# Gate and up projections of two feed-forwards by seven block products instead of eight

## The reference

```python
D_FF = ((8 * D_MODEL // 3 + 255) // 256) * 256        # 2816

def swiglu(x, w_gu, w_down):
    gu = x @ w_gu
    g, u = jnp.split(gu, 2, axis=-1)
    return (jax.nn.silu(g) * u) @ w_down

x = x + 0.5 * swiglu(rms_norm(x, g_ffn1[layer]), w_ffn1_gu[layer], w_ffn1_down[layer])
...
x = x + 0.5 * swiglu(rms_norm(x, g_ffn2[layer]), w_ffn2_gu[layer], w_ffn2_down[layer])
return rms_norm(x, g_final)
```

## Time and profile before

| | us |
|---|---|
| median of 3 runs | 1751.66 (1751.65 to 1751.79) |
| the profiled execution | 1754.53 |
| its span, first to last instruction | 1752.7 |
| PE busy in the span | 1742.0 (99%) |
| DVE / ACT / POOL busy | 1039.4 / 760.7 / 431.9 |

### The profile page before, as it was taken

One profiled execution on the slowest core, in us unless ns is written; L12 is line 12 of the kernel. 1 busy time (PEld: TensorE's weight loads), 2 busy tenths in 40 slices (PEclk: granted clock), 3 DMA queues, 4 the chain that ended last, 5 costly groups with the idle time before them and its releaser, 6 DMA issues.

```text
span 1752.7 us, 25465 instructions
## 1 busy us (share of the span) xinstructions
PE 1742.0 (99%) x9322; PEld 1437.8 (82%) x9322; DVE 1039.4 (59%) x2178; ACT 760.7 (43%) x1413; POOL 431.9 (25%) x336
## 2 busy tenths in 40 slices
PE   9999999999999999999999999999999999999998
PEld 7778878777888888888888888889888888888887
DVE  5888867688867665555433455446756655555332
ACT  6566645556654533333232454555444322333222
POOL 4566644465553500000000332320200200000000
PEclk9999999999999999999999999999999999999999
DMA  6422123332212433333333422223321333333332
GB/s 198 138 88 73 60 61 98 95 95 79 73 49 62 138 109 96 96 96 96 106 101 106 151 64 93 85 84 103 103 64 58 96 96 96 96 96 96 109 107 85
DMA packets 54998, 166.20 MB, mean 95 GB/s; under 512 B 10264, under 2 KB 10776, under 8 KB 54904
## 3 DMA queue, kind: packets, MB, share of 16 engines
q1 hardware_dynamic: 53896, 163.69, 30.8%
q10 hardware_dynamic: 1008, 1.28, 0.2%
HBM read 162.25 MB, written 2.17 MB: 94 GB/s over the span
## 4 chain that ended last, share of the span: by engine, by line
PE 99%; DMA 0%; DVE 0%; ACT 0%; POOL 0%; SPq 0%; issue 0%; POOLq 0%
PE proj L1182 80%; PE turned L1514 2%; PE o L1536 2%; PE proj L1678 1%; PE proj L1671 1%; PE o L1779 1%; PE o L1879 1%; PE turned L1148 1%; PE turned L1758 1%; PE score L1483 1%; PE score L1868 1%; PE turned L1741 1%; PE score L1472 1%; PE score L1348 0%; PE proj L1382 0%; PE score L1741 0%
## 5 line engine op out<-in xcount | busy, mean ns | idle before, releaser
L1182 PE MATMUL proj<-hhi,whi 128*128 128x512 f32 x1456 | 580.8, 399 | 0.0
L1182 PE MATMUL proj<-hhi,wlo 128*128 128x512 f32 x1456 | 568.4, 390 | 0.0
L1182 PE MATMUL proj<-hlo,whi 128*128 128x512 f32 x1456 | 567.4, 390 | 0.0
L1970 ACT ACTIVATE whi<-ring 128x1024 fp32r<-128x1024 f32 x278 | 294.2, 1058 | 613.6 <-PE proj L1182 593.8
L2495 DVE TENSOR_TENSOR wlo<-ring,whi 128x1024 fp32r<-128x1024 f32 x199 | 243.0, 1221 | 161.7 <-ACT whi L1970 161.2
L1182 PEld LDWEIGHTS proj<-hhi,whi 128*128 128x128 f32 x1456 | 274.0, 188 | 61.3 <-issue 7.3
L1182 PEld LDWEIGHTS proj<-hhi,wlo 128*128 128x128 f32 x1456 | 273.4, 188 | 58.8
L1182 PEld LDWEIGHTS proj<-hlo,whi 128*128 128x128 f32 x1456 | 274.1, 188 | 53.0
L884 POOL TENSOR_TENSOR wlo<-ring,whi 128x512 fp32r<-128x512 f32 x160 | 213.9, 1358 | 331.7 <-ACT whi L1970 331.4
L902 POOL TENSOR_TENSOR prob<-prob 128x512 f32<-128x512 f32 x36 | 56.8, 1579 | 871.2 <-ACT prob L1966 871.2
L1996 ACT ACTIVATE prob<-prob,negmax 128x128 f32<-128x128 f32 (+3 forms) x208 | 114.0, 550 | 80.5 <-DVE negmax L2568 80.1
(11 more groups left out here) (402 smaller groups left out, 2470.1 us busy)
## 6 DMA issues: line engine op xcount, KB each, us to landing
ring<-wstream SPq DMA_DIRECT2D x285, 512.0 KB, 3.6
arena<-lines SPq DMA_DIRECT2D x28, 256.0 KB, 5.4
out<-arena SPq DMA_DIRECT2D x8, 256.0 KB, 3.3
arena<-x ACTq DMA_DIRECT2D x4, 256.0 KB, 5.5
arena<-x SPq DMA_DIRECT2D x4, 256.0 KB, 6.2
arena<-mem SPq DMA_DIRECT2D x1, 1024.0 KB, 8.7
ring<-wstream SPq DMA_DIRECT2D x12, 64.0 KB, 2.3
ring<-wstream SPq DMA_DIRECT2D x2, 256.0 KB, 7.3
```

The costliest lines, as they stand in the source:

```text
L1182: mm = pe.matmul(b, rounded(w), rounded(rhs(v, k)), start=(first and n == 0 and p == 0), stop=(last and n == len(blocks) - 1 and p == 2))
L1970: act.activation(rounded(dst), src, ACT.Copy, scale=scale).then_inc(ready, 1)
```

## The change

Chunks 0 and 1 of each feed-forward stay as they are (PEEL = 2). For the other 20 (SEVEN), gate weights and up weights of a chunk are seen as one matrix of 2 x 2 blocks: gate and up by the first and second tile of each pair of input tiles. The normalised input, too, is 2 x 2 blocks: the two tiles of a pair by positions 0-255 and 256-511 (HALF_S). The product of these takes eight block products; the change uses the form with seven, in which some products are of sums of blocks:

- of weights: S1 (two up blocks), S2 (S1 and a gate block), S3 (gate and up), S4 (S2 and a gate block), made for every chunk by POOL in `seven_sums`; A11, A12 and A22 are used as they are,
- of inputs: T1 to T4 from `hx` (x times the gain, eight ACT copies in `scale_h`), made once per feed-forward by DVE (`combine_h`), rounded by ACT, low parts of T1 and T2 by POOL and of T3 and T4 by DVE.

Each of the seven products is 4 tile pairs x 3 parts = 12 matmuls of 128x256, in the order A11, S1, S2, A12, S3, S4, A22. Three banks hold the results: X (`proj`), Y (`score`), Z (`opsum`). X is continued by S2, S3 and A22, so ACT copies X after A11, S2 and S3 and Z after S1 (`q1c`, `v2c`, `v3c`, `q5c`), and DVE makes three adds. The high parts of the seven weight operands are made by ACT (`high_w`), the low parts of S2 and S3 by POOL, those of A11, S1, A12, A22 and S4 by DVE (`low_w`). The gating (`gated`) is done one chunk late. SP loads a chunk's two slots once DVE has made the low part of A22 of the chunk before last, not by jobs. `norm_first` goes behind the loop, and the loading of the first `bias2` rows (`load_bias2`) too.

```diff
+PEEL = 2
+SEVEN = FC - PEEL
+W_A11, W_S1, W_S2, W_A12, W_S3, W_S4, W_A22 = range(7)
+T_1, T_2, T_3, T_4 = range(4)
+HALF_S = S // 2
...
+        hx = over("hx", "arena", [P, KC, S], inner_at + 12 * S)
+        tsum, tlo = over("tsum", "yT", [P, 4, D]), over("tlo", "yT", [P, 4, D])
+        thi = over("thi", "arena", [P, 4, D])
+        c22 = over("c22", "arena", [P, HALF_S], 4 * D)
+        assert 4 * D + HALF_S <= inner_at
+        hhi_free = over("hhi_free", "hhi", [P, KC // 2, 2 * S])
+        ssum_free, slo_free = over("ssum_free", "hlo", [P, KC // 2, 2 * S]), over("slo_free", "hlo", [P, KC // 2, 2 * S])
+        q1c, q5c, v2c, v3c = (hhi_free[:, n, HALF_S:S] for n in range(4))
...
+        shi = {W_A11: unit("shi_a11", "whi", 0), W_S1: unit("shi_s1", "whi", 1),
+               W_A12: unit("shi_a12", "whi", 2), W_S3: unit("shi_s3", "whi", 3),
+               W_S2: unit("shi_s2", "prob", 0), W_S4: unit("shi_s4", "prob", 1), W_A22: unit("shi_a22", "prob", 2)}
+        ssum = {W_S1: unit("ssum_s1", "prob", 3), W_S2: unit("ssum_s2", "pT", 0), W_S3: unit("ssum_s3", "pT", 1),
+                W_S4: ssum_free[:, :, HALF_S:HALF_S + P]}
+        slo = {W_S1: unit("slo_s1", "prob", 3), W_S2: unit("slo_s2", "pT", 0), W_S3: unit("slo_s3", "pT", 1),
+               W_S4: slo_free[:, :, HALF_S:HALF_S + P], W_A22: slo_free[:, :, HALF_S + P:S],
+               W_A11: unit("slo_a11", "pT", 2), W_A12: unit("slo_a12", "pT", 3)}
...
-                with sp.Fori(0, FC // 2) as i:
+            def load_ffn(n0, j0, f):
+                for s in range(4):
+                    sp.wait_ge(job_done, j0 + s + 1)
+                    load(stream_of(n0) + s + RING, s)
+                with sp.Fori(1, FC // 2) as i:
                     for s in range(4):
-                        sp.wait_ge(job_done, i * 4 + (j0 + s + 1))
+                        if s % 2 == 0:
+                            sp.wait_ge(slo_ready, i * 10 + (SLO + 5 * (f * SEVEN + s // 2 - 2) + 4))
...
+                pool.wait_ge(wload[up], i * 16 + 16 * (n0 // RING + 1 + s))
+                if not ahead:
+                    pool.wait_ge(sop_done, i * 12 + (SOP + 6 * (g - 1) + W_S1 + 1))
+                pool.tensor_tensor(ssum[W_S1], weight_quarter(up, 1), weight_quarter(up, 2), ALU.add).then_inc(sum_made, 1)
+                pool.wait_ge(wload[gate], i * 16 + 16 * (n0 // RING + 1 + s))
+                pool.wait_ge(sum_made, i * 8 + (SUM + 4 * g + 1))
+                if not ahead:
+                    pool.wait_ge(sop_done, i * 12 + (SOP + 6 * (g - 1) + W_S2 + 1))
+                pool.tensor_tensor(ssum[W_S2], ssum[W_S1], weight_quarter(gate, 1), ALU.add).then_inc(sum_made, 1)
+                if ahead:
+                    low_t(f, T_2)
+                else:
+                    pool.wait_ge(sop_done, i * 12 + (SOP + 6 * (g - 1) + W_S3 + 1))
+                pool.tensor_tensor(ssum[W_S3], weight_quarter(gate, 1), weight_quarter(up, 1), ALU.add).then_inc(sum_made, 1)
+                pool.wait_ge(sum_made, i * 8 + (SUM + 4 * g + 2))
+                if ahead:
+                    pool.wait_ge(job_done, j0 + 2 * PEEL)
+                else:
+                    pool.wait_ge(sop_done, i * 12 + (SOP + 6 * (g - 1) + W_S4 + 1))
+                pool.tensor_tensor(ssum[W_S4], ssum[W_S2], weight_quarter(gate, 2), ALU.add).then_inc(sum_made, 1)
+                pool.wait_ge(sum_made, i * 8 + (SUM + 4 * g + 4))
+                for w in (W_S2, W_S3):
+                    pool.wait_ge(shi_ready, i * 14 + (SHI + 7 * g + w + 1))
+                    pool.tensor_tensor(slo[w].bitcast(F32R), ssum[w], shi[w], ALU.subtract).then_inc(pool_slo_ready, 1)
...
+                    def product(to, w, parts, first):
+                        for k in range(KC // 2):
+                            for p, (weight, v) in enumerate(((shi[w], parts[0]), (shi[w], parts[1]), (slo[w], parts[0]))):
+                                mm = pe.matmul(to, rounded(weight[:, k, :]), rounded(v[:, k, :]), start=(first and k == 0 and p == 0),
+                                               stop=(k == KC // 2 - 1 and p == 2), skip_group_check=True)
+                        return mm
...
+                    pe.wait_ge(job_free[b], i * 2 + (j0 + s) // 2)
+                    pe.wait_ge(slo_ready, i * 10 + (SLO + 5 * g + 1))
+                    product(X, W_A11, h11, True).then_inc(sop_done, 1)
+                    pe.wait_ge(slo_ready, i * 10 + (SLO + 5 * g + 2))
+                    pe.wait_ge(pool_tlo_ready, PTLO + 2 * f + 1)
+                    product(Z, W_S1, t1, True).then_inc(sop_done, 1)
+                    pe.wait_ge(pool_slo_ready, i * 4 + (PSLO + 2 * g + 1))
+                    pe.wait_ge(pool_tlo_ready, PTLO + 2 * f + 2)
+                    pe.wait_ge(qc_ready, i * 8 + (QC + 4 * g + 1))
+                    product(X, W_S2, t2, False).then_inc(sop_done, 1)
+                    pe.wait_ge(slo_ready, i * 10 + (SLO + 5 * g + 3))
+                    product(Y, W_A12, h21, True).then_inc(sop_done, 1)
+                    pe.wait_ge(pool_slo_ready, i * 4 + (PSLO + 2 * g + 2))
+                    pe.wait_ge(tlo_ready, TLO + 2 * f + 1)
+                    pe.wait_ge(qc_ready, i * 8 + (QC + 4 * g + 3))
+                    product(X, W_S3, t3, False).then_inc(sop_done, 1)
+                    pe.wait_ge(slo_ready, i * 10 + (SLO + 5 * g + 5))
+                    product(Z, W_S4, h22, False).then_inc(sop_done, 1)
+                    pe.wait_ge(slo_ready, i * 10 + (SLO + 5 * g + 4))
+                    pe.wait_ge(tlo_ready, TLO + 2 * f + 2)
+                    pe.wait_ge(qc_ready, i * 8 + (QC + 4 * g + 4))
+                    product(X, W_A22, t4, False).then_inc(job_done, 2)
...
+                def body(i, s, first=False, last=False):
+                    g = f * SEVEN + s - 2
+                    b, Z = proj[(j0 + s) % 2], opsum[s % 2]
+                    def copy(src, dst, done):
+                        act.wait_ge(sop_done, i * 12 + (SOP + 6 * g + done + 1))
+                        act.activation(dst, src[:, 0:HALF_S], ACT.Copy).then_inc(qc_ready, 1)
+                    if first:
+                        high_w(W_A22, 0, 1)
+                    else:
+                        high_w(W_A22, i, s - 1)
+                        act.wait_ge(gate_scaled, i * 2 + (GATED + g))
+                        tanh_of((s - 1) % 2, -0.5)
+                    copy(b, q1c, W_A11)
+                    if not last:
+                        high_w(W_A11, i, s)
+                    copy(Z, q5c, W_S1)
+                    if not first:
+                        high_inner(i * 2 + (s - 1), (s - 1) % 2)
+                    copy(b, v2c, W_S2)
+                    if last:
+                        act.activation(rowsum[:, 0:1], rowsum[:, 0:1], ACT.Copy).then_inc(hi_ready, 2 * SEVEN)
+                        act.wait_ge(wload[0], 16 * ((n0 + 2 * FC) // RING + 1))
+                        make_high(0, 0)
+                    else:
+                        for w in (W_S1, W_S2, W_A12):
+                            high_w(w, i, s)
+                    copy(b, v3c, W_S3)
...
+                        for w in (W_S3, W_S4):
+                            high_w(w, i, s)
...
-                        dve.wait_ge(tanh_ready, c + (DEPTH * 8 + f * FC + 1))
-                        dve.scalar_tensor_tensor(tmp[:, s, :], tanh[:, s, :], 1.0, tmp[:, s, :], ALU.add, ALU.mult)\
-                            .then_inc(ffn_step, 1)
-                        dve.wait_ge(job_done, i * 4 + (j + 2))
-                        dve.wait_ge(ffn_step, c + (f * FC + 1))
-                        dve.tensor_tensor(tmp[:, s, :], tmp[:, s, :], proj[(j + 1) % 2][:, :], ALU.mult)\
-                            .then_inc(job_free[(j + 1) % 2], 1)
-                        dve.wait_ge(job_free[(j + 1) % 2], i * 2 + ((j + 1) // 2 + 1))
-                        dve.tensor_tensor(tmp[:, s, :], tmp[:, s, :], R[:, :], ALU.mult).then_inc(inner_done, 1)
-                        make_low((2 * s + 3) % RING, 1, i * 4 + (s0 + 2 * s + 4))
...
+                def gated(i, s):
+                    b, h = (j0 + s) % 2, s % 2
+                    dve.wait_ge(job_done, i * 4 + (j0 + 2 * s + 2))
+                    dve.wait_ge(tanh_ready, i * 2 + (s + DEPTH * 8 + f * FC + 1))
+                    dve.scalar_tensor_tensor(tanh[:, h, 0:HALF_S], tanh[:, h, 0:HALF_S], 1.0, proj[b][:, 0:HALF_S], ALU.subtract, ALU.mult)\
+                        .then_inc(job_free[b], 2)
+                    dve.scalar_tensor_tensor(tanh[:, h, HALF_S:S], tanh[:, h, HALF_S:S], 1.0, c22[:, :], ALU.subtract, ALU.mult)\
+                        .then_inc(ffn_step, 1)
+                    dve.wait_ge(ffn_step, i * 2 + (s + f * FC + 1))
+                    dve.tensor_tensor(tmp[:, h, :], tanh[:, h, :], tmp[:, h, :], ALU.mult).then_inc(wg_step, 1)
+                    dve.wait_ge(wg_step, i * 2 + (s + f * SEVEN - PEEL + 1))
```

(33 more changed lines are left out.)

252 lines of the change are left out of this document (203 added, 49 removed).

## The result

| | before | after |
|---|---|---|
| median, us | 1751.72 (4 runs, 1751.65 to 1752.78) | 1879.26 (4 runs, 1878.08 to 1879.74) |
| profiled execution, span | 1752.7 | 1877.3 |
| mean granted clock | 0.998 | 0.973 |

The ratio is 1.0726, 95% interval 1.0707 to 1.0744: 7% slower, 21 us above the forecast of 1858 and inside its range.

The account below looks back on a forecast made before the run. PE bounds the kernel before; the resource DVE and POOL share would bound the loop. Per feed-forward 20 x (13.4 - 10.9) = 50, plus 3 for entry and exit; two make 106: 1858 us, range 1815 to 1900.

Parts of the forecast that it names:

- PE alone: Seven-product chunk on PE: 84 matmuls at 0.1196 us, 10.05 us, 0.83 less than 10.88.
- the 0.23 for a start: Possible extra at a product's first matmul behind a wait; at all seven, 1.6 us a chunk; forecast took 10.05 without it.
- The shared resource: DVE operations with two SBUF inputs and POOL operations exclude each other, released 0.14 us early: floor 12.4 us a chunk.
- Six waits: DVE waits six times a chunk for POOL, 5.5 us together; with 7.8 of its own, 13.4 us a chunk.
- the low parts' long durations: Sign in the profile after: DVE lows of 128x512 near 1.2 us on average instead of 0.69.
- the upper end: Chunk without overlap between DVE operations and with six full waits: 8.8 + 5.8 = 14.6 us, 1906 in all.
- the other signs: Loop profile after: POOL operations near 1.6 to 1.8 us instead of 1.29, DVE busy for over 90%.
- PE's waits: PE waits some 0.6 us at the third product and 2.7 at the fifth, which needs ACT's copy.
- The clock: Rival: PE's pauses lower the clock; whole loop +305 us, a quarter some 50; 6% for anything above 1900.
- Entry: First of the 20 chunks takes 4.3 us more, low parts of T in POOL's queue; scaled copies of x nothing.
- Exit: Behind the last of the 20 chunks, 1.2 us come back.
- Rival 1: DVE and POOL pass each other in the loop, PE stays the bound: 10.06 us a chunk, 1725 in all; 6%.

Follow-up runs that it names:

- a_psum: Changed kernel, but each of a chunk's eleven DVE operations with two SBUF inputs takes one from PSUM, output wrong: 1736.5 us.
- b_warm: Changed kernel plus sixteen unread 128x256 matmuls in front of the waits of each chunk's fifth product: 1859.0 us.
- b_late: Changed kernel plus sixteen unread 128x256 matmuls behind the waits of each chunk's fifth product: 1940.9 us.
- a_lows: Changed kernel, but only the five DVE low parts of the weights take one input from PSUM, output wrong: 1860.2 us.
- e_rpsum: Changed kernel, but a chunk's two DVE multiplications by R read R from its PSUM bank instead of the SBUF copy: 1805.4 us.
- g2_cf: Changed kernel with R, X's copy behind S3, c22 and two gating results in PSUM, and ACT's copy behind S2 before rounding inner: 1777.4 us.

## Why the prediction was right, and where its sizes were off

The forecast was 106 us more; measured were 124.6 between the profiled executions and 127.5 between the medians. The mechanism was the one forecast; the sizes were off in both directions.

- **PE alone, 10.05 a chunk, and its gain of 0.8:** right. a_psum shows 10.08. The low price of 0.1196 for 256 columns held with all seven starts; the 0.23 for a start didn't occur.
- **The shared resource, released 0.14 before the recorded end:** right. In the rows of 710 it is 0.15 (the two rows at 578 and 579, as printed, give 0.15 too). The Trainium skill (SBUF — State Buffer, "Who interferes with whom") says that a DVE instruction with two SBUF inputs contends with POOL's reads and one with at most one SBUF input, outside DVE's two-port modes, doesn't; the trace agrees, 1182 ns against 414 in a_psum for the same step. That the pair is held for the whole instruction the page says of DVE's two-port modes; the prediction carried this over to operations with two SBUF inputs. It would make 14.8 a chunk against 13.0 measured with a full clock; the measurement decides for the earlier release.
- **Six waits, 5.5 us, and 13.4 a chunk:** with the clock kept up it was 13.01 (b_warm). In the changed kernel DVE does wait for POOL at six places, five of them among those named: the scaling of the gate 0.70 (forecast 0.63), the second and third steps of the gating 0.77 and 0.97 (0.75 and 0.97), the add into `c22` 0.92 (1.09), each its row above less the time that it takes alone. The low of A22 began later and waited 0.37 instead of 1.09 (a row of 1045 ns). The sixth is the last step of the gating, 0.95, in place of the low of A12 (0.99), which waited not at all (676 ns). Sum 4.7 instead of 5.5; read the same way in b_warm, with the full clock, 4.8 (rows of 1334, 1182, 1662, 1507, 1038 and 1667 ns). The prediction had 2.1 of the waits in low parts, where 0.4 is, and so named the low parts' long durations as a sign; that sign did not come. In return DVE, which by the prediction never rests, waits in every chunk for ACT's rounding of A22 (b_warm, 700 to 850):

```profile
DVE slo_free L3189 <- ACT shi_a L2491: 8.0, 12, 0.7
```

That is 0.67 a chunk instead of the 0.3 allowed for waits on others: 7.5 + 0.7 + 4.8 = 13.0. The chunk was 0.4 too high: 36 chunks x 0.4 = 14 us too much. (The 8.8 of the upper end is 0.2 more than its terms, 8.3 and 0.3, give; nothing else uses it.) Of the other signs, POOL's operations took 1.51 in the mean from 700 to 850 (forecast near 1.6 to 1.8), and DVE was busy for 89% of the loop (over 90).

- **PE's waits:** 2.7 at the fifth product, released by ACT's copy: measured 2.66, by the same, or 2.35 behind a slowed chunk. The 0.6 at the third isn't there.
- **The clock:** this is the step that was mis-sized. I made it a rival, at 6%, and wrote that the granted clock would still be 1.00. It was 0.92 in the loop. The trace of before had no such pause in dense work, only the stretch of tiny matmuls, and I took that for the nearest row and argued that PE streams for three quarters of a chunk. It does, and the clock fell all the same. b_warm, with the pause filled, keeps 1.00, and b_late, with as many matmuls behind it, does not. Whether it is the single pause or the share of time in which PE works that decides, no run separates: every kernel whose clock fell in the loop has both longer pauses and a smaller share of matmul work in a chunk than every kernel whose clock held. Cost 0.73 a chunk, 26 us. Rows at either level would have priced it: 3.4 us at 0.21 instead of 0.12 a matmul is 1.5 us for each fall, of which a part comes back in the chunk behind it (12.67 against 13.01).
- **Entry:** the first chunks were forecast 4.3 above 13.4, that is 17.7, and took 17.83 and 18.22. But in chunks 0 and 1 I had priced only the scaled copies of x, and left out that DVE's four sums of T stand ahead of its low parts there. The chain in the first feed-forward, and then what PE waited for in the second (1440 to 1485):

```profile
618.06 1.14 DVE tsum L3164
...
625.60 2.22 DVE wlo L2742
...
627.96 5.72 PE proj L1290 x24
```

```profile
PE proj L1290 <- DVE wlo L2742: 3.8, 2, 2.3
```

Chunk 2 began 3.4 us later than before in the first feed-forward (633.5 against 630.1), and in the second the delay grew by another 4.3 over chunks 0 and 1: some 8 us that the sum put at nothing.

- **Exit:** the last of the 20 chunks, from its first matmul to the first of the down jobs, was forecast 1.2 below 13.4, that is 12.2, and took 10.7 in both (898.64 to 909.34, 1734.60 to 1745.31): 3 us less.

Together: -14 for the pace, +26 for the clock, +1 in the first chunks, +8 at the entries and -3 at the exits make 18, and 124.6 - 106 is 18.6. Between the medians, 1858 and 1879, it is 21: I had taken off 2.9 by which the profiled execution of the kernel before lay above its median, and that of the changed kernel (1879.14) did not lie above its own. The forecast was near in part by luck, because errors had opposite signs. Rival 1 (DVE and POOL pass each other) did not occur, but a_psum shows that its price was right within 12 us: 1736 against 1725.

## What to carry to other kernels

Before work is given to idle engines, add up what they share: here each engine had room by its own count, and what broke was one resource between DVE and POOL. A DVE operation that read one of its two inputs from a PSUM bank took nothing of it (a_psum), and which operations are moved there matters more than how many: first those on whose result another engine waits. When a change makes PE pause in dense work for the first time, price the clock as well, and read it again whenever the pause changes.

## What the runs showed of the hardware that I had not expected

- PE's pauses of up to 2.7 us in the changed kernel were followed by a granted clock of 0.50 for some 3.4 us behind 9 of 13 of them, those of 1.8 to 1.9 us in a_lows behind 13 of 14, those of 2.35 in b_late behind 5 of 12, while in b_warm (0.8), e_rpsum (1.4) and g2_cf (1.6) the clock stayed at 1.00. What besides the pause decides, PE's share of work among other things, is open.
- DVE's time for 128x512 doesn't depend on where its second input lies when POOL is quiet: 0.68 to 0.70 from SBUF or PSUM, with the result in SBUF or PSUM.
- POOL and DVE alternate strictly where both want in: in the changed kernel three DVE operations in a row took 1.18, 1.66 and 1.64 beside POOL operations of 1.74, 1.47 and 1.51 (0.69 and 1.29 alone, 0.41 for the first of the three).
